# The eight piece moves of each shifted state-space table go out on ACT's queue in place of SP's

## The reference, cut to what matters

```python
_, _, xr, xi = lax.associative_scan(combine, (ar_t, ai_t, bu_re, bu_im), axis=1)
y = (jnp.einsum('gcp,bsgp->bsgc', c_re.astype(f32), xr)
     - jnp.einsum('gcp,bsgp->bsgc', c_im.astype(f32), xi))
y = y.reshape(B, S, W) + d_skip.astype(f32) * u.astype(f32)
y = jax.nn.gelu(y).astype(u.dtype)
return y * jax.nn.sigmoid(y @ glu_w + glu_b)
```

## Time and profile before

| | before |
|---|---|
| median of 3 runs | 1342.96 us (1342.22 to 1343.66) |
| the profiled execution | 1341.15 us, its span 1339.3 us |
| TensorE busy | 1269.4 us, 95% of the span |
| DVE, ACT, POOL busy | 63%, 39%, 36% |
| mean granted clock of TensorE | 0.978 of full speed |
| chain that ended last, by engine | PE 75%, SP's queue 6%, ACT 5%, DVE 5%, DMA 5%, issue 3% |

### The profile page before, as it was taken

One profiled execution on the slowest core, in us unless ns is written; L12 is line 12 of the kernel. 1 busy time (PEld: TensorE's weight loads), 2 busy tenths in 40 slices (PEclk: granted clock), 3 DMA queues, 4 the chain that ended last, 5 costly groups with the idle time before them and its releaser, 6 DMA issues.

```text
span 1339.3 us, 16564 instructions
## 1 busy us (share of the span) xinstructions
PE 1269.4 (95%) x6240; PEld 1022.0 (76%) x6240; DVE 847.4 (63%) x1360; ACT 516.1 (39%) x862; POOL 487.9 (36%) x344
## 2 busy tenths in 40 slices
PE   7899999999989999989989999999999899999997
PEld 3687688787768877868756876887877688788886
DVE  5777777876468865874463768778657688442241
ACT  5254313753425333423233532156443333433321
POOL 1243232343525224544403432323443332245551
PEclk9999999999989999989989999999999899799999
DMA  9342121132132336562435311211320423344312
GB/s 357 120 142 79 48 78 49 48 110 79 48 110 65 88 87 210 178 243 79 155 138 197 111 60 47 69 58 48 128 79 14 126 67 86 103 135 164 94 63 79
DMA packets 64176, 142.05 MB, mean 106 GB/s; under 512 B 31200, under 2 KB 31328, under 8 KB 63328
## 3 DMA queue, kind: packets, MB, share of 16 engines
q1 hardware_dynamic: 63040, 138.89, 31.7%
q10 hardware_dynamic: 1056, 2.10, 0.4%
HBM read 128.12 MB, written 10.49 MB: 103 GB/s over the span
## 4 chain that ended last, share of the span: by engine, by line
PE 75%; SPq 6%; ACT 5%; DVE 5%; DMA 5%; issue 3%; POOL 1%; DVEq 0%; ACTq 0%
PE bank L1672 20%; PE bank L1673 19%; PE bank L1674 19%; PE bank L1860 4%; DMA raw<-in_wfull 3%; SPq L700 2%; SPq L727 2%; SPq L691 2%; PE bank L1821 1%; PE bank L1684 1%; PE bank L1831 1%; PE bank L1845 1%; DVE ada L1141 1%; PE bank L1930 1%; ACT w_hi L794 1%
## 5 line engine op out<-in xcount | busy, mean ns | idle before, releaser
L760 POOL TENSOR_TENSOR w_lo<-raw,w_hi 128x512 fp32r<-128x512 f32 (+1 forms) x170 | 244.4, 1438 | 831.5 <-ACT w_hi L794 831.5
L1672 PE MATMUL bank<-h_hi,w_hi 128*128 128x512 f32 x896 | 365.3, 408 | 17.5 <-POOL w_lo L761 15.4
L1674 PE MATMUL bank<-h_hi,w_lo 128*128 128x512 f32 x896 | 351.8, 393 | 0.0
L1673 PE MATMUL bank<-h_lo,w_hi 128*128 128x512 f32 x896 | 351.3, 392 | 0.0
L794 ACT ACTIVATE w_hi<-raw 128x1024 fp32r<-128x1024 f32 (+2 forms) x170 | 178.4, 1052 | 303.9 <-DMA raw<-in_wfull 168.4
L761 POOL TENSOR_TENSOR w_lo<-raw,w_hi 128x512 fp32r<-128x512 f32 (+2 forms) x170 | 251.2, 1478 | 0.0
L1672 PEld LDWEIGHTS bank<-h_hi,w_hi 128*128 128x128 f32 x896 | 170.1, 190 | 60.8 <-POOL w_lo L761 18.8
L1673 PEld LDWEIGHTS bank<-h_lo,w_hi 128*128 128x128 f32 x896 | 170.1, 190 | 39.1 <-issue 5.0
L1674 PEld LDWEIGHTS bank<-h_hi,w_lo 128*128 128x128 f32 x896 | 169.6, 189 | 36.5
L1672 PE MATMUL bank<-w_hi,h_hi 128*128 128x512 f32 (+1 forms) x256 | 99.3, 388 | 11.3 <-POOL w_lo L761 5.0
L1673 PE MATMUL bank<-w_lo,h_hi 128*128 128x512 f32 (+1 forms) x256 | 97.1, 379 | 0.0
(11 more groups left out here) (275 smaller groups left out, 1798.4 us busy)
## 6 DMA issues: line engine op xcount, KB each, us to landing
raw<-in_wfull SPq DMA_DIRECT2D x178, 512.0 KB, 3.6
arena<-in_wada SPq DMA_DIRECT2D x40, 512.0 KB, 5.5
x_scratch<-xm SPq DMA_DIRECT2D x2, 2048.0 KB, 8.3
arena<-x_scratch SPq DMA_DIRECT2D x2, 2048.0 KB, 9.7
arena<-in_x SPq DMA_DIRECT2D x4, 512.0 KB, 5.9
arena<-in_s5m SPq DMA_DIRECT2D x2, 1024.0 KB, 6.5
u_scratch<-arena ACTq DMA_DIRECT2D x2, 1024.0 KB, 4.3
arena<-u_scratch SPq DMA_DIRECT2D x64, 32.0 KB, 1.9
```

What stands on the lines that cost most here:

```text
L760: nc.gpsimd.tensor_tensor(lo[:, :half], raw_chunk(n)[:, :half], hi[:, :half].bitcast(F32), ALU.subtract)
L1672: mm(out_, a_hi, b_hi, start=first, stop=False)
L1673: mm(out_, a_hi, b_lo, start=False, stop=False)
L1674: return mm(out_, a_lo, b_hi, start=False, stop=last)
```

## The change

The block of part 2 that issues the eight pieces moves, waits and all, from SP's program to ACT's, at the same step of the list. Nothing else is touched.

```diff
@@ in block.sync
-                if kind == "s5" and step[3] == 2:
-                    j, key = step[2], step[:3]
-                    wait_read(sp, (key, 0))
-                    wait_read(sp, (key, 1))
-                    sp.wait_ge(mt_clear, l + 1)
-                    if j >= 2:
-                        wait_read(sp, (("s5", l, j - 2), 7))
-                    for jj in range(CH):
-                        sp.dma_start(mt2[j % 2][jj * GC:(jj + 1) * GC, :, jj * GC:P],
-                                     kt[0:GC, :, 0:(CH - jj) * GC]).then_inc(mt_in, 16)
@@ in block.scalar, behind the s5 parts 1 and 4
+                if kind == "s5" and step[3] == 2:
+                    j, key = step[2], step[:3]
+                    wait_read(act, (key, 0))
+                    wait_read(act, (key, 1))
+                    act.wait_ge(mt_clear, l + 1)
+                    if j >= 2:
+                        wait_read(act, (("s5", l, j - 2), 7))
+                    for jj in range(CH):
+                        act.dma_start(mt2[j % 2][jj * GC:(jj + 1) * GC, :, jj * GC:P],
+                                     kt[0:GC, :, 0:(CH - jj) * GC]).then_inc(mt_in, 16)
```

## The result

| | before | after |
|---|---|---|
| median | 1342.64 us (1342.22 to 1343.66, 4 runs) | 1327.79 us (1326.62 to 1329.49, 4 runs) |
| the profiled execution | 1341.15 us, span 1339.3 us | 1329.49 us, span 1327.7 us |
| mean granted clock of TensorE | 0.978 | 0.981 |

The ratio is 0.9889, with a 95% interval from 0.9872 to 0.9906: 1.1% faster. The median fell by 14.9 us where 15.2 us were forecast, but the profiled execution fell by only 11.66 us, so the terms have to be looked at one by one. (Lines above the moved block keep their numbers; behind it L794 became L783, L760 and L761 became L750 and L751, L997 and L998 became L986 and L987, L1007 became L996, L1019 became L1008. The pieces are now L1019, on ACT's queue.)

The account below looks back on a forecast made before the run. TensorE, busy 95%, was held to idle in gaps because weight chunks queued behind the pieces on SP. 2.34 + 0.54 + 2.5 + 3.25 + 6.56 = 15.2 us off 1342.96 gave 1327.8 us; own range 1324 to 1331, whole range 1323 to 1338.

Parts of the forecast that it names:

- The mechanism: SP's queue: without eight pieces ahead, the weight chunk goes out 5.1 to 6.1 us earlier each turn, closing TensorE's gaps.
- Gaps of 2.34 and 0.54 us: First layer, turn 2: TensorE's idle before part 4 and before swap L1935; both close, -2.34 and -0.54 us.
- of 2.74 us: First layer, behind turn 3: TensorE's gap at 527.84 closes by a hair, so counted as -2.5 us.
- the sum for the first layer: First layer's three gap terms together: 2.34, 0.54 and 2.5 us saved.
- Second layer, 3.25 and 6.56 us: Second layer, turn 2: the gap before part 4 closes, -3.25 us, and the half clock behind it goes, -6.56 us.
- nothing new is waited for: ACT's queue: the waits moved with the pieces are on ACT's own earlier work or long done, costing nothing.
- The fourth rival: Behind 485: half-clock stretches elsewhere fall otherwise, costing half their length, moving the end 1.6 us; no chance of its own.
- No fall of the clock: Second layer, behind part 4 of turn 2: with no gap ahead, the clock should not fall, saving 6.56 us.
- The first rival: SP and ACT issues take turns, lengthening L691 and L700 by 5.1 us a turn; gaps stay, 1343 us; chance 0.14.
- independent: SP's and ACT's queues: issuing at once does not hinder either, each issue having a fixed sequencer price.
- When the pieces go out: ACT's queue: pieces of turns 1 to 3 begin near 436, 464 and 489, at 0.6 us each.
- the plain transfer L979: Nearest row of ACT's queue, 0.37 to 0.39 us, used for the low end of eight issues' cost, 3.0 us.

Follow-up runs that it names:

- Experiment 1: Kernel after, pieces still on ACT, plus eight unread transfers of nearly the pieces' form per turn in SP's old place; 1344.26 us, ratio 0.9997.
- experiment 2: Kernel before, all pieces still on SP but issued behind the next weight chunks instead of ahead; 1326.29 us, ratio 0.9869.
- experiment 5: Kernel after, with ACT waiting in turns 1 to 3 until the previous turn's store has landed before issuing its pieces; 1326.42 us, ratio 0.9866.
- experiment 4: Kernel after, but only the second layer's pieces on ACT, the others back on SP; 1334.85 us, ratio 0.9936.

## Why the prediction was right, and where its terms were not

*The mechanism* stands: a weight chunk that leaves SP's queue some 5 us sooner closes the gaps behind it. Experiment 1 takes the whole gain back by filling SP's place alone, and experiment 2 has it without ACT.

*Gaps of 2.34 and 0.54 us, and of 2.74 us.* All three closed. The trace is 5.47 us ahead by 589.98, and the sum for the first layer was 5.38. The third, counted as 2.5 because it would close by a hair, closed fully.

*Second layer, 3.25 and 6.56 us.* Both went, but 1.57 us came back as the wait for the store, a term that the forecast put at nothing: "nothing new is waited for" looked at the moved waits only, not at the waits that stay and that a layer without the gap and without the half clock meets at other moments. The table of experiment 5 shows that the pieces beside the store are not what made it. 3.25 + 6.56 - 1.57 = 8.24 against 8.14 in the trace and 8.6 in experiment 4.

*Half-clock stretches elsewhere.* The fourth rival gave them 1.6 us either way, and the profiled execution gave back 1.93 us between 589.98 and 1053.24. Not all of the 13.7 us between 683 and 718 did that. Behind the first stretch ACT's splits are still 5.45 us ahead (708.91 against 714.36), behind the second 3.75 us (724.31 against 728.06): its 3.4 us cost half their length, 1.7 us, since TensorE was busy all through them. In the first it was busy for 7.30 of 10.3 us, and the longer half clock cost nothing that the splits show. So half the length, which the rival took, holds only where TensorE has no idle time. With the 1.57 us this is why the profiled execution gained 11.66 us and not 15.2. The medians gained 14.9; that this hits the forecast to 0.3 us is partly luck, since terms of 1.6 and 1.9 us were missed, and each kernel's own runs scatter by 1 to 3 us here and by more in the later runs of the kernel before.

*"No fall of the clock" from the length of the gap.* The forecast set the first layer's gap, with clock 1.00 behind it, against the second layer's. The trace before had it so, but experiments 1 and 4 show the fall behind 2.09, 2.40 and 2.91 us, while none follows the gap of 2.74 us at 527.84 in the trace before. For the change it made no difference, because the gaps went altogether; for a change that only shortened them it might have.

*Queues taking turns.* The first rival is out: L657 left SP 5 us sooner. But the queues are not independent either, as the forecast took them. These are SP's eight L691 wholly beside ACT's issues (experiment 5), alone (before), and alone with a fetch packet on the same microseconds (experiment 2):

```profile
488.91 4.69 SPq L691 DMA_DIRECT2D arena<-y_scratch  x8
...
494.78 3.64 SPq L691 DMA_DIRECT2D arena<-y_scratch  x8
...
459.60 5.06 SPq L691 DMA_DIRECT2D arena<-y_scratch  x8
```

Beside ACT's issues six of the eight took 0.59 to 0.63 us and not 0.43 us, 1.05 us together, where that rival wanted 5.1 us a turn. The 5.01 us at 462.60 in the kernel after are only in part that: one of its eight issues took 1.29 us, with a fetch packet starting at 464.14, and in experiment 2, where ACT issues no pieces, one took 1.85 us with such a packet. Of the 16 issues' 9.21 us (462.60 to 471.81, 7.84 before) 0.86 us is that one issue. The Trainium skill ("Perfetto Trace Analysis", section "DMA Instruction — HWDGE (DVE, Sync)") describes one descriptor generator that each sequencer locks, with the wait counted in the issue's duration. That fits the longer issues here; if the lock is the reason, 0.16 to 0.20 us on top of 0.43 us say that it is held for only part of an issue, which no run here tests.

*When the pieces go out.* The forecast had turns 1 to 3 begin near 436, 464 and 489, the first behind the sine. They began at 432.70, 462.21 and 487.44; why is told below.

## What to carry to other kernels

An engine that waits for a transfer may really wait for the queue ahead of it: eight small transfers landed in some 2.2 us each but held the queue for 5 us, and 16 held it for 7.4. Put the transfer that the bounding engine will miss first ahead of runs of small ones; here that order alone was worth 1.3% and, applied to the inputs too, 2.7%, and a second issuing queue was not needed for either. Before writing "nothing new is waited for", list the landings that other engines wait for and how much later each may come: here one store had 0.9 us in hand over its 2.0 us, and when it came later than that, TensorE waited.

## What the runs showed that was not expected

**ACT's queue issues ahead of ACT's work.** In the program the pieces of turn 1 stand behind the eviction L1008, the table load and both sines. In the trace the first issue of L1019 is at 432.70, while L1008 has been running only since 432.61, and the sines follow at 434.52 and 435.05. These transfers, whose own semaphores were set, did not wait for the engine's earlier work. It is why the pieces ran beside the store (issued at 433.23), and where one must come behind ACT's work it needs a semaphore for it, as in experiment 5.

**A store that took 2.0 us became 2.7 to 4.5 us.** Pieces in flight beside it account for 0.7 to 0.9 us (gone in experiment 5), and a 16 KB packet of instruction fetch lay beside every one of more than 3.3 us.

**The spread of an issue's price.** The rows of L1019 over the whole profile:

```profile
L1019 ACTq DMA_DIRECT2D arena<-arena x64: 557/622/1591, 404.6 to 1149.3; - x64
```

On ACT's queue the piece took 622 ns in the median, on SP's 600 ns, so for this form the queue hardly matters, and the plain transfer L979 was indeed the wrong row to take for it.
